# Values' products two passes behind scores, combination in even passes, and three instructions of VectorE moved up

## What is computed

```python
# layers 0, 1: mixer (A: recurrence, B: state space, C: spatial gating)
rec = causal_dwconv(rec_a); u = mult * (i * rec); h = scan(a, u)      # mult = sqrt(-expm1(2 log a))
ya = h * gelu(gate_a)
yb = rms_norm((ssd(...) + x_c * d_skip) * silu(z))
yc = u * (w_s @ layer_norm(v) + b_s)                                   # after gelu
m = concatenate([ya, yb, yc]) @ w_out
# third block: attention, 8 heads of 64, 2 key/value heads
vc = gelu(blocks(v_cmp) @ cmp_w1[1]) @ cmp_w2[1]                       # compressed values
o_cmp = masked_softmax(q @ kc) @ vc
o_sel, o_win = softmax(q @ k) @ v                                      # two masks, two key sets
o = g0 * o_cmp + g1 * o_sel + g2 * o_win
# third block: state space, 32 groups of 64 states
y = real(scan(lam_bar, u @ b_bar) @ c) + d * u
```

## Time and profile before

| | profiled execution | |
|---|---|---|
| device time | 1493.72 us | median of three runs 1492.43 us |
| span of the trace | 1491.8 us | first to last instruction |
| TensorE, products | 1466.2 us | 98% |
| TensorE, weight loads | 1273.6 us | 85%, beside products |
| VectorE | 1147.2 us | 77% |
| ScalarE | 772.3 us | 52% |
| GpSimd | 143.0 us | 10% |
| DMA | 261.75 MB | 175 GB/s |
| TensorE's granted clock, mean | 0.991 | 1.0 is 2.4 GHz, 0.5 is 1.2 GHz |

### The profile page before, as it was taken

The page is one execution under the profiler, slowest core; times in us unless marked ns, Lnnn a source line. Parts: engine busy times, 40 slices in busy tenths (PEclk is TensorE's granted clock), DMA queues, the critical chain, the costliest instruction groups (busy, mean ns, idle before and its releaser), DMA issues.

```text
span 1491.8 us, 24498 instructions
## 1 busy us (share of the span) xinstructions
PE 1466.2 (98%) x8583; PEld 1273.6 (85%) x8583; DVE 1147.2 (77%) x1833; ACT 772.3 (52%) x1260; POOL 143.0 (10%) x140
## 2 busy tenths in 40 slices
PE   8999999999999999999999999999899999999999
PEld 7888889888888888889978888898787799888887
DVE  5787777877778777787787777878699877567776
ACT  6334376564344543447655434477488765453432
POOL 0000024100000000004220000011333310000000
PEclk9999999999999999999999999999799999999999
DMA  8656555546656665565456665566322256646662
GB/s 317 200 191 197 183 170 170 156 154 199 191 189 197 213 198 190 192 196 167 132 169 192 198 195 187 167 184 226 99 85 72 86 167 187 184 155 195 195 189 83
DMA packets 71361, 261.75 MB, mean 175 GB/s; under 512 B 8048, under 2 KB 8048, under 8 KB 71024
## 3 DMA queue, kind: packets, MB, share of 16 engines
q1 hardware_dynamic: 69984, 253.79, 53.8%
q10 hardware_dynamic: 1296, 6.85, 1.3%
HBM read 259.56 MB, written 1.05 MB: 175 GB/s over the span
## 4 chain that ended last, share of the span: by engine, by line
PE 90%; DVE 5%; ACT 3%; issue 1%; POOL 0%; DMA 0%; ACTq 0%; DVEq 0%
PE work L762 25%; PE work L763 12%; PE acc L475 9%; PE acc L477 9%; PE acc L476 9%; PE work L475 7%; PE work L477 7%; PE work L476 7%; DVE wlo L461 2%; PE work L1488 1%; ACT whi L454 1%; PE acc L1517 1%; PE acc L1553 1%; PE work L1489 0%; PE work L1476 0%
## 5 line engine op out<-in xcount | busy, mean ns | idle before, releaser
L461 DVE TENSOR_TENSOR wlo<-raw,whi 128x1024 fp32r<-128x1024 f32 x460 | 550.4, 1223 | 188.4 <-ACT whi L454 187.1
L762 PE MATMUL work<-xboth,whi 128*128 128x512 f32 x1600 | 560.8, 394 | 0.0
L454 ACT ACTIVATE whi<-raw 128x1024 fp32r<-128x1024 f32 x480 | 476.0, 1040 | 64.2 <-PE work L477 36.0
L763 PE MATMUL work<-xboth,wlo 128*128 128x256 f32 x1600 | 444.3, 278 | 0.0
L762 PEld LDWEIGHTS work<-xboth,whi 128*128 128x128 f32 x1600 | 299.8, 187 | 69.3
L763 PEld LDWEIGHTS work<-xboth,wlo 128*128 128x128 f32 x1600 | 300.8, 188 | 4.3
L840 ACT ACTIVATE sg<-sg 128x256 f32<-128x256 f32 x100 | 41.8, 418 | 476.0 <-DVE sg L881 476.0
L477 PE MATMUL acc<-whi,hlo 128*128 128x512 f32 x440 | 173.7, 395 | 0.0
L476 PE MATMUL acc<-wlo,hhi 128*128 128x512 f32 x440 | 173.5, 394 | 0.0
L475 PE MATMUL acc<-whi,hhi 128*128 128x512 f32 x440 | 173.3, 394 | 0.0
L475 PE MATMUL work<-xboth,whi 128*128 128x256 f32 x416 | 120.4, 290 | 0.0
(11 more groups left out here) (438 smaller groups left out, 2207.4 us busy)
## 6 DMA issues: line engine op xcount, KB each, us to landing
raw<-stream SPq DMA_DIRECT2D x480, 512.0 KB, 3.7
par<-pm ACTq DMA_DIRECT2D x2, 1644.5 KB, 7.5
pfa<-pf_a ACTq DMA_DIRECT2D x3, 516.0 KB, 3.9
pfb<-pf_b ACTq DMA_DIRECT2D x2, 516.0 KB, 8.5
x<-x_in SPq DMA_DIRECT2D x2, 512.0 KB, 5.8
out<-x SPq DMA_DIRECT2D x4, 256.0 KB, 2.0
par<-pm ACTq DMA_DIRECT2D x1, 820.0 KB, 4.3
pre<-pf_a ACTq DMA_DIRECT2D x1, 4.0 KB, 4.0
```

Source lines behind the costliest of these rows:

```text
L454: nc.scalar.activation(chunk(whi, place, c)[:, cols], chunk(raw, place, c)[:, cols], ACT.Copy).then_inc(hi_ready, 1)
L461: nc.vector.tensor_tensor(chunk(wlo, place, c)[:, cols], chunk(raw, place, c)[:, cols], chunk(whi, place, c)[:, cols].bitcast(F32), ALU.su ...
L762: nc.tensor.matmul(o[:, :], hi[:, k * P:(k + 1) * P], xboth[:, k, :], start=k == 0, stop=False)
L763: m = nc.tensor.matmul(o[:, 0:S], lo[:, k * P:(k + 1) * P], xhi[:, k, :], start=False, stop=k == KD - 1)
```

## The change

VectorE's list of emptied tiles and its order change for `cmp1`: it is emptied right after the compressed key's mean square, ahead of the low part of chunk 35. Values' products come two passes behind scores instead of one: in pass r, from the third pass on, TensorE makes those of r - 2, and after the last pass those of 14 and 15. `combine` runs in passes 6, 10 and 14. In the layers' mixers, the low part of chunk 21 comes ahead of `mult2`, and the first low part of the turned yb ahead of the multiplication of the second tile by u.

```diff
-BY_DVE2 = ["cv1", "cv2", "cv4", "cmp1", "cv5", "cs0", "cs1", "cv7", "bu0"]
+BY_DVE2 = ["cv1", "cv2", "cmp1", "cv4", "cv5", "cs0", "cs1", "cv7", "bu0"]
@@ passes: order of TensorE's reports
-    JOBS2 += (_new if _r % 4 != 3 else _new[:1]) + _cmp[0] + _turn + _cmp[1] + ([f"pv{_r - 1}"] if _r else []) + ([f"y5{_r - 1}"] if _r and _r % 2 == 0 else [])
+    JOBS2 += (_new if _r % 4 != 3 else _new[:1]) + _cmp[0] + _turn + _cmp[1] + ([f"pv{_r - 2}"] if _r >= 2 else []) + ([f"y5{_r - 1}"] if _r and _r % 2 == 0 else [])
-JOBS2 += ["pt15", "pv15", "y515"] + _ots
+JOBS2 += ["pt15", "pv14", "pv15", "y515"] + _ots
@@ mix_dve
+            split_lo(dve, place, [C_UV + 3])
             mult2.inc(nc.vector.scalar_tensor_tensor(out=th[:, :, :], in0=rg[:, :, :], scalar=1.0, in1=th[:, :, :], op0=ALU.add, op1=ALU.mult))
-            split_lo(dve, place, [C_UV + 3])
             weights(1)
...
+            def low_part(b):
+                y_hi.wait(dve, 2 + b)
+                y_lo.inc(nc.vector.tensor_tensor(ylo[:, 3 + b, :], bank(f"ybt{b}", slice(0, S)), yhi[:, 3 + b, :].bitcast(F32), ALU.subtract))
...
+                if t == 1:
+                    low_part(0)
                 vec.wait(dve, vec.k)
                 yc_ready.inc(nc.vector.tensor_tensor(yc[:, t, :], yc[:, t, :], uv[:, t, 0:CW], ALU.mult))
-            for b in range(AB):
-                y_hi.wait(dve, 2 + b)
-                y_lo.inc(nc.vector.tensor_tensor(ylo[:, 3 + b, :], bank(f"ybt{b}", slice(0, S)), yhi[:, 3 + b, :].bitcast(F32), ALU.subtract))
+            low_part(1)
+            low_part(2)
@@ mix2_pe
-                    values(r - 1)
+                    if r >= 2:
+                        values(r - 2)
...
             turn(15)
+            values(14)
             channel(24)
             values(15)
@@ mix2_dve
+            job2.wait(dve, JOB2["cmp1"])
+            emptied("cmp1", tt(vcs, bank2("cmp1", slice(0, HD)).unsqueeze(1).broadcast_to([P, 8, HD]), bc(mask8[:, :], HD), ALU.mult))
             split_lo(dve, place, [35])
             conv_low(0)
             conv(4)
 
             nrm.wait(dve, 3)
-            job2.wait(dve, JOB2["cmp1"])
-            emptied("cmp1", tt(vcs, bank2("cmp1", slice(0, HD)).unsqueeze(1).broadcast_to([P, 8, HD]), bc(mask8[:, :], HD), ALU.mult))
...
-                if r % 4 == 1 and r > 1:
+                if r % 4 == 2 and r > 2:
                     combine(r // 4 - 1)
```

## The result

The changed kernel took 1484.35 us (median of five executions, 1482.49 to 1486.97), the kernel before 1492.43. The ratio is 0.9943, with a 95% interval of 0.9932 to 0.9954: 8.5 us less, between 6.9 and 10.1. The profiled execution took 1482.49 us, which is 11.2 less than the profiled one before, but only because it is the fastest of its five; 8.5 is the figure to explain.

The account below looks back on a forecast made before the run. TensorE was taken as the bound, busy 1466.2 of 1491.8 us, leaving only its 25.6 us of standing still and clock losses to win. Entrance 6.1 + passes 3.3 + low parts 1.6 = 11.0 us, so 1481.4 us; range 1476.5 to 1486.5.

Parts of the forecast that it names:

- Early emptying: Third block's mixer entrance: 4.0 us of wait before query transposes and 2.1 us behind it go, 6.1 us together.
- The key is no new wait: Mixer entrance: TensorE reaches the normalised compressed key at 1054.9, after it is ready just behind 1054.36; no added wait.
- The second half-clock stretch: Behind the eight-column products of compressed scores: stays, 0 us gained; bounds 0 to 4.3 us.
- Rival 2: Clock stays up through compressed scores: gain 15.3 us, time 1477.1, or 1474.4 with passes at upper bound; chance 0.12.
- The passes: Last block's passes: 9.6 us to win, less 4.8 and 1.5, gives 3.3 us; bounds 0.5 to 6.
- Waits for the weights: Passes, before values' products: 2.4 us of waits for turned weights go, as their copy has a whole pass more.
- The wait of 1.67 us becomes about 1: Passes, before the next scores: the wait shrinks because exponentials of pass 7 start about 1.3 us earlier.
- ScalarE without a gap in gelu pairs: Two pass pairs with a gelu: ScalarE needs 16.48 us, TensorE 14.09; 2.4 us stay lost in each, 4.8 us.
- Half clock in these waits costs nothing more: Passes: no added loss from half clock, because TensorE then waits for ScalarE anyway.
- The combination's weight ahead of odd maxima: Passes 7, 11 and 15: 0.5 us left lost for each of three, 1.5 us.
- Low parts: Two layers' mixers: one of two waits goes, 0.8 us a layer, 1.6 us; bounds 0.8 to 3.3.
- Rival 1: The passes give nothing; gain 6.1 + 1.6 = 7.7 us, time 1484.7; chance 0.18.

Follow-up runs that it names:

- Bank alone: The kernel before with only the earlier emptying of compressed values' bank (`cmp1`): 1488.45 us, ratio 0.9970.
- the four later versions in block form: Changed kernel, compressed scores in one block, with combination behind next maximum (1479.8 us), copy for gelu (1479.4), gelu two passes sooner (1480.3), or first and third together (1479.9).
- the mixed order: The changed kernel with the eight-column products of compressed scores laid between the wide products of the following channel chunk: 1490.6 us.
- values alone: The kernel before with only values' products two passes behind scores, combination left in odd passes: 1491.45 us, ratio 0.9993.
- the two experiments on the gelu: The changed kernel with a copy in place of the state-space gelu, 1479.4 us; and with that gelu two passes sooner on ScalarE, 1480.3 us.
- low parts alone: The kernel before with only the low parts moved in the two layers' mixers: 1491.4 us, ratio 0.9994.
- passes alone: The kernel before with only values' products two passes behind and the combination in even passes: 1491.4 us, ratio 0.9991.
- behind: The changed kernel with the combination behind the next scores' maximum instead of ahead of it, its scratch in another tile: 1479.8 us, ratio 0.9916.
- sooner: The changed kernel with the state-space gelu in passes 5, 9 and 13 instead of 7, 11 and 15: 1480.3 us, ratio 0.9913.
- combination alone: The kernel before with only the combination moved to even passes, values' products one pass behind as before: 1490.0 us, ratio 0.9970.

## Why the prediction was right, and where it was not

**Early emptying.** Right in its mechanism: the emptying took 0.67 us beside GpSimd, at 1048.89 where the forecast put it, and TensorE's 16 transposes ran through. The 0.3 us kept for a stretch by GpSimd weren't needed. The Trainium skill (GPSIMD Engine Reference, Key points) names two SBUF inputs, or a mode with two ports, as what brings VectorE's instructions into contention with GpSimd; the emptying has one SBUF input, and 0.67 us agrees. "The key is no new wait" was off by a little: VectorE's L2047 ended at 1054.74, and TensorE waited 0.36 us for it and 0.27 for its copy; before, the copy had 0.40. Compressed scores start 6.5 us earlier, for a forecast of 6.1. In both profiles TensorE begins the query transposes at the same moment (1048.68 and 1048.69, since the gain in the layers and a longer half-clock stretch at the 24-column products cancel), so all 6.5 us are the step's in this pair of profiles. The old stretch scatters, though: 13.12 us before, 11.92 to 12.94 in the four other profiles that have it, against 6.64 to 6.67 in all new ones, 5.9 us in the mean.

**What that is worth at the end.** The step that was over-sized is counting 6.1 us at the entrance as 6.1 us of the kernel. Bank alone gave 4.5 (3.1 to 6.0). Two things stand against the 6.1, and the runs don't say how much each took: up to the first scores the new entrance is shorter by 5.3 us in the mean of the profiles, not 6.1, and behind it waits for the turned weights grew from 2.4 to 4.1 us. In the whole change these waits are gone too: the rest of the three parts alone fell by 2.1 + 1.1 + 1.7 = 4.9 us, that of the whole by 7.2.

**The second half-clock stretch.** Left in place at no gain, and it stayed, behind compressed scores and with TensorE busy in all of them. Its length is a matter of the execution: from the first eight-column product to the first scores the two profiles of the changed kernel have 8.24 and 9.80 us, bank alone 9.80, the four later versions in block form 8.22 to 9.85; with the old entrance it is 8.2 in four profiles and 11.03 in the kernel before. Taking away the gap ahead of it, the emptying didn't make it shorter. (The prediction's price of 4.3 us for it is a little high by its own rows: 3.40 / 18 less 1.40 / 13 is 0.08 us a product, not 0.1, so 3.9; its sum doesn't use it.) Rival 2, and with it what the Trainium skill says of gaps as the cause (TensorE: Matmul & The Clock Gate, HAM oscillation — how this bites in real kernels), is not what this place shows: with the gap of 4.3 us gone the half clock came all the same, though gaps of 0.36 and 0.27 us are left ahead of it, and in the mixed order it lasted longer, with TensorE busy all the while. In the passes the half clock did lie behind waits, of 0.5 to 1.7 us, but in three other profiles waits as long had none behind them, so a wait alone doesn't decide it there either.

**The passes, 3.3 us forecast.** By time they gave 1.3 (0 to 2.8), inside the bounds of 0.5 to 6 but less than half the value taken. Its parts:

- Waits for the weights "go": 2.4 to 0.4 us, right. But values alone showed that they had hidden waits for exponentials, which grew to 5.9.
- "The wait of 1.67 us becomes about 1": 1.11, right.
- ScalarE without a gap in gelu pairs, 16.5 us: in the pair from 1115.56 to 1133.88 it took 18.3, of which 1.85 idle behind VectorE's maximum, so 16.5 busy. The term is right, and the two experiments on the gelu confirm that it costs 4 to 5 us.
- "Half clock in these waits costs nothing more, because TensorE then waits for ScalarE anyway" is the step that failed. It was partly true of the old order, where pass 8 lasted 9.64 us with a short half-clock stretch and 9.63 at full clock; but it lasted 11.06 with a longer one, and pass 10 lasted 9.64 instead of 8.10. That is 1.5 us of time for half clock in the passes of the kernel before and 1.4 in those of low parts alone. In the new order TensorE has no values' products to wait for: ScalarE was done with the exponentials of pass 8 at 1128.97, and TensorE came for the next scores only at 1130.83, 1.9 us later, for its clock. Counted like this, half clock cost the passes 2.2 and 3.4 us in the two profiles of the changed kernel and 3.6 in that of passes alone, 1 to 2 us more than in the old order. This fits the 2.0 us of the passes' gain that are missing, and that both cures (behind, sooner) give more than half of their gain by the clock (3.3 of 4.8 us, 2.2 of 4.0, by the means).
- The combination's weight ahead of odd maxima, 1.5 us: moving it behind gave 4.6 (1.6 rest, 3.3 clock). Under-sized for the same reason.

**Low parts, 1.6 us forecast.** One of two waits gone, the other kept at 0.75 us a layer, as forecast; rest 1.7 us less. The total of 0.9 by time doesn't contradict it, nor would it alone have shown it.

**The sum.** 11.0 forecast, 8.5 measured (6.9 to 10.1). By time the entrance was over by 1.6 us, the passes by 2.0, low parts by 0.7, and the whole gives 1.8 more than its parts alone (6.7), a difference that lies within the noise of four measurements. The bounds of the terms held. Rival 1's time (1484.7) is nearer to the median than the forecast's, and half of its mechanism is there: the passes alone give little. Its other half isn't, since it has the entrance at its full 6.1.

**Open.** Why combination alone loses less by the clock (8.7 us in the mean) than combination with values (12.2); how the 1.6 us that bank alone lacks are shared; and where and how long the clock falls at the 24-column products in any one execution.

## What to carry to other kernels

Cost a wait on TensorE twice: by its own length, and by the half clock that may follow, which counts in full where TensorE, not another engine, then has the next thing to finish; here the second part was up to twice the first. Before you count a wait as won, look at what the same engine would have waited for next, since a stop that hides another gives back only their difference. And where executions scatter by their clock, compare mean times split by the granted clock, not two profiles: 11.2 us between the two profiles here were 8.5 between the kernels.

## What the runs showed of the hardware that I had not expected

- Waits of only 0.75 to 1.1 us on TensorE are followed by stages at clock 0.50 (1.2 GHz), as at 1122 behind the wait of 1.11 us, and a wait of 0.75 us before pass 10 in "behind" was followed by none; nor were the waits of up to 1.7 us in the profiles of bank, values and combination alone. What decides it isn't shown.
- Eight-column products mixed with 256-column ones, with TensorE busy for 2.00 of 2.00 us in each stage from 1056 on, ran at half clock for some 13 us, longer than in a block of their own.
- The same kernel's mean granted clock goes from 0.991 to 0.993 between executions, and for the mixed order from 0.987 to 0.992, which is 1486.45 to 1492.61 us.
- VectorE's instruction L2088 on 128 x 8 values took 1.06 us in the changed kernel and 0.17 in "behind". In the timelines of GpSimd and VectorE of the changed kernel it ends, to 0.02 us, with a GpSimd instruction on 128 x 512 values that had begun before it:

```profile
1115.05 1.29 POOL L1899 TENSOR_TENSOR rotated<-g,par 128x512 f32<-128x512 f32 x1 [4.46 <-DVE g L2130]
1115.30 1.06 DVE L2088 TENSOR_TENSOR rs<-rs,ngate 128x8 f32<-128x8 f32 x1
```

  In "behind" the same happens to L2086 (0.83 instead of 0.14 us, until 1118.98; GpSimd's L1900 from 1117.66 lasts until 1118.96). So the small first steps of a combination can cost 0.7 to 0.9 us more than their size says.
